# Sums of squares, norm spreads and bonus sums of a layer 0 projection in array tiles of a quarter

## What is computed

```python
qkv = silu(causal_dwconv(f[..., :1536], conv_w))          # 12 blocks of 128 channels: q, k, v
q, k = l2norm(heads(q, 128)) * 128 ** -0.5, l2norm(heads(k, 128))
f = f + (f_prev - f) * mu                                  # r, k, v, wd, ad, gd of the other group
w_log = -softplus(-(w0 + tanh(wd) @ w2)) - 0.5             # lora of the decay
a = sigmoid(a0 + ad @ a2)                                  # lora of the gate
kk = l2norm(heads(k * k_k, 64))
k = k * (1 + (a - 1) * k_a)
bonus = sum(r_h * k_h * r_k, axis=-1) * v_h
```

## Time and profile before

| | |
|---|---|
| median of 3 runs | 1567.32 us (1565.9 to 1569.51) |
| span of the profiled execution | 1565.6 us; its time beside the span is not listed apart |
| TensorE busy | 1492.0 us, 95% of the span |
| VectorE, ScalarE, POOL busy | 844.8, 666.4, 91.4 us |
| mean granted TensorE clock | 0.981 of 2.4 GHz |

### The profile page before, as it was taken

The page is one execution under the profiler, slowest core; times in us unless marked ns, Lnnn a source line. Parts: engine busy times, 40 slices in busy tenths (PEclk is TensorE's granted clock), DMA queues, the critical chain, the costliest instruction groups (busy, mean ns, idle before and its releaser), DMA issues.

```text
span 1565.6 us, 24908 instructions
## 1 busy us (share of the span) xinstructions
PE 1492.0 (95%) x9901; PEld 1243.9 (79%) x9901; DVE 844.8 (54%) x1400; ACT 666.4 (43%) x1156; POOL 91.4 (6%) x132
## 2 busy tenths in 40 slices
PE   5999998999999999999999997999989999999997
PEld 4776776887778888878888986988868888878886
DVE  4366546777676442334436626787746442334433
ACT  5543434445545442124334434676645442124331
POOL 0110013322300000000000002000000000000000
PEclk8999999999999999999999998999999999999999
DMA  6222200000152233322331241000042323322321
GB/s 224 81 70 78 81 14 14 2 2 2 55 189 76 99 94 110 95 81 94 108 122 55 81 139 64 2 2 3 2 135 68 93 93 110 95 81 94 108 81 54
DMA packets 32607, 119.38 MB, mean 76 GB/s; under 512 B 3696, under 2 KB 3824, under 8 KB 32496
## 3 DMA queue, kind: packets, MB, share of 16 engines
q1 hardware_dynamic: 29808, 108.84, 21.7%
q10 hardware_dynamic: 2688, 8.98, 1.6%
HBM read 115.71 MB, written 2.10 MB: 75 GB/s over the span
## 4 chain that ended last, share of the span: by engine, by line
PE 74%; DVE 8%; ACT 3%; issue 1%; DMA 0%; ACTq 0%; DVEq 0%; SPq 0%
PE bank L337 19%; PE bank L339 18%; PE bank L338 18%; PE bank L2543 2%; PE bank L2556 2%; PE bank L1136 2%; PE bank L2532 1%; PE bank L2533 1%; PE bank L1118 1%; PE bank L1082 1%; PE bank L2135 1%; DVE nmax L2613 1%; PE bank L1022 1%; PE bank L1126 1%; DVE ul_m L459 1%
## 5 line engine op out<-in xcount | busy, mean ns | idle before, releaser
L330 DVE TENSOR_TENSOR wl_m<-ring,wh_m 128x1024 fp32r<-128x1024 f32 x124 | 152.0, 1226 | 158.5 <-ACT wh_m L322 156.2
L337 PE MATMUL bank<-uh_m,wh_m 128*128 128x512 f32 (+2 forms) x576 | 216.5, 376 | 3.6 <-DVE ffo L1946 1.9
L338 PE MATMUL bank<-ul_m,wh_m 128*128 128x512 f32 (+2 forms) x576 | 216.0, 375 | 0.0
L339 PE MATMUL bank<-uh_m,wl_m 128*128 128x512 f32 (+2 forms) x576 | 216.0, 375 | 0.0
L322 ACT ACTIVATE wh_m<-ring 128x1024 fp32r<-128x1024 f32 x124 | 131.6, 1061 | 192.2 <-PE bank L339 189.7
L337 PE MATMUL bank<-wh_m,hh 128*128 128x512 f32 x448 | 174.4, 389 | 0.0
L338 PE MATMUL bank<-wl_m,hh 128*128 128x512 f32 x448 | 174.3, 389 | 0.0
L339 PE MATMUL bank<-wh_m,hl 128*128 128x512 f32 x448 | 174.3, 389 | 0.0
L1936 DVE TENSOR_TENSOR hraw<-hraw 128x512 f32<-128x512 f32 x64 | 44.3, 693 | 166.7 <-ACT hraw L1892 166.6
L1892 ACT ACTIVATE hraw<-bank 128x512 f32<-128x512 f32 x64 | 38.3, 598 | 214.8 <-PE bank L339 214.8
L337 PEld LDWEIGHTS bank<-uh_m,wh_m 128*128 128x128 f32 x576 | 108.6, 189 | 24.9 <-issue 2.7
(11 more groups left out here) (418 smaller groups left out, 2809.1 us busy)
## 6 DMA issues: line engine op xcount, KB each, us to landing
ring<-in_wstream_dram SPq DMA_DIRECT2D x200, 512.0 KB, 3.5
rowbuf<-in_rows_dram ACTq DMA_DIRECT2D x6, 512.0 KB, 3.8
xres<-in_x_dram SPq DMA_DIRECT2D x4, 512.0 KB, 6.7
xres<-in_x_dram ACTq DMA_DIRECT2D x1, 2048.0 KB, 10.0
out_dram<-xres ACTq DMA_DIRECT2D x4, 512.0 KB, 4.5
prerow<-in_rows_dram ACTq DMA_DIRECT2D x3, 512.0 KB, 4.9
con<-in_consts_dram SPq DMA_DIRECT2D x1, 869.5 KB, 13.3
par<-in_params_dram SPq DMA_DIRECT2D x1, 680.5 KB, 11.7
```

Source lines behind the costliest of these rows:

```text
L330: v.sig(v.e.tensor_tensor(dn[3][:, c % RING, :], slot(c), dn[2][:, c % RING, :].bitcast(F32), ALU.subtract), sem("w_lo"), it * per + c + 1)
L337: pe.matmul(out, lh, rh, start=start, stop=False)
L338: pe.matmul(out, lh, rl, start=False, stop=False)
L339: return pe.matmul(out, ll, rh, start=False, stop=stop)
```

## The change

- The two loras run in two blocks, in front of chunks 4 and 5. Each has two gate products on the rows 64 to 127 of the array and two decay products on the rows 0 to 63 by turns, in four banks. The gate's sigmoid and the decay's sum are made in halves, in steps 4 and 5, and the decay's sigmoid in step 6.
- The squares run in three groups, in front of chunks 10, 19 and 23: four products of 32 columns of weights, each into another quarter of the partitions of the bank. ScalarE puts the squares in four buffers that are free then (the values' slots, and the bonus operand's), and waits for a sum only once in four. Roots and reciprocals run on 128 partitions in place of 8; lines without a sum hold a root of eps.
- The key norms' spreads run as one group in front of chunk 15, into banks 7, 4, 5 and 6: four products of 32 rows with the high halves, then four with the low ones. Those of q and k are such a group each, in front of chunks 27 and 28. The eight rows of the selector that POOL copied shrink to three, from a new constant.
- The bonus sums are four products of 32 columns (`bonus_sums`, in front of chunk 12) that leave the sums with time along the columns. ScalarE copies them to SBUF (step 12, behind `root_hi`), four transposes turn them (`turn_bonus`, in front of chunk 13), and VectorE copies the columns that count in step 14.
- `turn_ba`, the gate steps and sums move one chunk later, and VectorE's `normed` of the keys too.

The diff, cut to its core:

```diff
-        sq = xres[:, 2, :].rearrange("p (b t) -> p b t", b=2)
+        bT = xres[:, 2, 0:T]
-        LW_BANK = (5, 6, 7, 4)
+        ALORA_BANK, LW_BANK = (4, 5, 4, 5), (6, 7, 6, 7)
+        KEY_BANK = (7, 4, 5, 6)
+        def sq(j):
+            return rk[:, j - 8, :] if j >= 8 else F(VRB + j % 4)
+        def quad(q):
+            return slice(32 * q, 32 * q + 32)
...
         def proj0_pe(pe):
+            def loras(i):
+                if i == 0:
...
+                    pe.wait_ge(sem("wd_tanh"), 1)
+                else:
+                    pe.wait_ge(sem("a_done"), i)
+                    pe.wait_ge(sem("lw_in"), i)
+                for b in (i, i + 1):
+                    pe.matmul(bank[ALORA_BANK[b]][:, :], PR("w2a2")[64:128, b * P:(b + 1) * P], fT[64:128, WA, PAD:],
                               start=True, stop=True).then_inc(sem("a_ready"), 1)
+                    pe.matmul(bank[LW_BANK[b]][:, :], fT[0:64, WA, PAD + b * P:PAD + (b + 1) * P], PR("w2a2")[0:64, :],
                               start=True, stop=True).then_inc(sem("lw_ready"), 1)
...
+            def squares(g):
+                pe.wait_ge(sem("sq_done"), 4 * g + 4)
...
+                window = C("rows2") if g == 0 else C("row")[:, g - 1:g + 31]
+                for q in range(4):
+                    ins = pe.matmul(bank[6 if g == 0 else 7][quad(q), :], window, sq(4 * g + q), start=g < 2, stop=g != 1)
+                ins.then_inc(sem("ss_ready"), 1)
+            def spread_norms(g):
+                if g < 2:
+                    pe.wait_ge(sem("inv_norm"), g + 1)
+                if g == 0:
                     pe.wait_ge(sem("by_pool"), 1)
                     pe.wait_ge(sem("gate_step"), 5)
                     pe.wait_ge(sem("bonus_sb"), 1)
+                for n in (nrh, nrl):
+                    for q in range(4):
+                        if n is nrh and g:
+                            pe.wait_ge(sem("normed"), 4 if g == 1 else 5 + q)
+                        ins = pe.matmul(bank[KEY_BANK[q] if g == 0 else 4 + q][:, :], spread[quad(q), g, :], n[quad(q), :], start=n is nrh, stop=n is nrl)
+                        if n is nrl:
+                            ins.then_inc(sem("spread"), 1)
+            def bonus_sums():
                 pe.wait_ge(sem("rk_done"), 4)
+                pe.wait_ge(sem("gate_step"), 2)
+                for b in range(4):
+                    ins = pe.matmul(bank[4][quad(b), :], C("rows2"), rk[:, b, :], start=True, stop=True)
+                ins.then_inc(sem("bonus_ready"), 1)
+            def turn_bonus():
+                pe.wait_ge(sem("bonus_ready"), 2)
                 for i in range(NT):
+                    ins = pe.transpose(bank[4][:, i * P:(i + 1) * P], bT[:, i * P:(i + 1) * P], ident)
                 ins.then_inc(sem("bonus_ready"), 1)
...
         def proj0_dve(v):
...
+                if p == 14:
+                    e.wait_ge(sem("bonus_ready"), 3)
+                    e.tensor_copy(bonus[:, :, :].rearrange("p i (b c) -> p i b c", c=2),
+                                  bank[4][:, :].rearrange("p (i b x) -> p i b x", i=NT, b=4)[:, :, :, 15:17]).then_inc(sem("bonus_sb"), 1)
+                if 15 <= p < 19:
+                    normed(p - 15)
...
         def proj0_pool(g):
+            e.wait_ge(sem("con_loaded"), 16)
+            e.tensor_copy(spread[:, 0, :].rearrange("p (h c) -> p h c", h=2), C("quad")[:, 0:2].unsqueeze(2).to_broadcast([P, 2, 64]))
+            e.tensor_copy(spread[:, 1:3, :], C("quad")[:, 0:3:2].unsqueeze(2).to_broadcast([P, 2, P])).then_inc(sem("by_pool"), 1)
...
         def proj0_act(a):
...
                 if p == 11:
-                    gate_exps()
                     root(1)
                 if p == 12:
+                    gate_exps()
                     root_hi(1)
+                    e.wait_ge(sem("bonus_ready"), 1)
+                    e.activation(bT, bank[4][:, :], ACT.Copy).then_inc(sem("bonus_ready"), 1)
```

More of the change, by code:

```diff
@@ L70 @@
 CONST_PARTS = [("ident", P), ("eps", 4), ("ones", P), ("strict", P), ("incl", P), ("bones", P), ("cum", 2 * P),
-               ("pairs", P), ("same", (LEVELS - 1) * 64), ("row", 31), ("rows2", 32), ("neg", P), ("cmask", NT * NCMP), ("cneg", NT * NCMP),
+               ("pairs", P), ("same", (LEVELS - 1) * 64), ("row", 36), ("quad", 3), ("rows2", 32), ("neg", P), ("cmask", NT * NCMP), ("cneg", NT * NCMP),
                ("ifreq", HALF), ("hsel", 4)]
@@ L197, in program @@
         early = ExitStack()
-        spread = sb("spread", [P, 12, P], F32R, c=early)
-        nr = sb("nr", [8, T], c=early)
+        spread = sb("spread", [P, 3, P], F32R, c=early)
+        nr = sb("nr", [P, T], c=early)
         early.close()
@@ L578, in gate_sums @@
                 pe.matmul(bank[5][:, 16:32].rearrange("p (i h) -> p i h", i=NT), ones, gs[:, :, 0, :], start=True, stop=True).then_inc(sem("gate_step"), 1)
[L580 to L588, removed]
+            def squares(g):
+                pe.wait_ge(sem("sq_done"), 4 * g + 4)
+                if g == 0:
+                    pe.wait_ge(sem("lw_in"), 4)
+                elif g == 1:
+                    pe.wait_ge(sem("normed"), 1)
+                window = C("rows2") if g == 0 else C("row")[:, g - 1:g + 31]
+                for q in range(4):
+                    ins = pe.matmul(bank[6 if g == 0 else 7][quad(q), :], window, sq(4 * g + q), start=g < 2, stop=g != 1)
+                ins.then_inc(sem("ss_ready"), 1)
@@ L621, in proj0_pe @@
                     gate_sums()
-                if p == R0 + 6:
-                    bonuses()
-                if R0 + 7 <= p < R0 + 11:
-                    spread_norm(p - R0 - 7)
-                if CONV0 + 4 <= p < CONV0 + 12:
-                    squares(4 + p - CONV0 - 4)
+                    squares(0)
+                if p == 12:
+                    bonus_sums()
+                if p == 13:
+                    turn_bonus()
+                if p == 15:
+                    spread_norms(0)
@@ L628, in proj0_pe @@
+                if p in (19, 23):
+                    squares(1 if p == 19 else 2)
                 weights(pe, p)
@@ L637, in z_products @@
                     if c < NTB + 2:
-                        for j in range(4):
-                            spread_norm(4 + 4 * (c - NTB) + j)
+                        spread_norms(1 + c - NTB)
                     weights(pe, c)
@@ L675, in conv, with log_decay @@
                     v.link(ins) if i < 3 else ins.then_inc(sem("conv_done"), 1)
-            def log_decay():
-                for i in range(NT):
+            def log_decay(first):
+                for i in (first, first + 1):
                     e.wait_ge(sem("lw_ready"), i + 1)
@@ L800, in key_norm, with a_gate @@
                 square(b, kkT[:, b, :])
-            def a_gate():
-                for b in range(4):
+            def a_gate(first):
+                for b in (first, first + 1):
                     e.wait_ge(sem("a_ready"), b + 1)
-                    e.activation(aT[:, b, :], bank[4 + b][:, :], ACT.Sigmoid, bias=PR("a0")[:, b:b + 1]).then_inc(sem("a_done"), 1)
+                    e.activation(aT[:, b, :], bank[ALORA_BANK[b]][:, :], ACT.Sigmoid, bias=PR("a0")[:, b:b + 1]).then_inc(sem("a_done"), 1)
             def log_decay():
```

90 lines of the change are left out of this document (31 added, 59 removed).

## The result

The changed kernel took 1548.79 us (median of 5 runs, 1545.11 to 1552.19), the kernel before 1566.91 us on the same chip (median of 5). The ratio is 0.9875 with a 95% interval of 0.986 to 0.989. The forecast of 1546.3 us is 0.9866 of the 1567.32 it started from, inside that interval.

A forecast was written before the change was run, and what follows sets the result against it. TensorE was taken as the bound, with insertions between projection chunks paid in full. Savings 3.4 + 10.5 - 0.1 + 1.4 - 0.45 + 6.2 = 20.95 us off the median 1567.3 gave 1546.3 us (chance 0.42), range 1542 to 1555.

The forecast's parts named there:

- Loras: Two blocks in front of chunks 4 and 5, four passes each, 2.2 us a block: saved 3.4 us.
- Squares: Twelve single squares become three groups of 1.27 us, four column quarters running at once: saved 10.5 us.
- rival 2: Square and spread groups: quarters run two at a time, 3.9 us more, 1550.2 us; chance 0.11.
- rival 3: Column tiles run one after another, a square group 3.77 us, three cost 7.5 more, 1553.8 us; chance 0.08.
- Gates: Gate steps one chunk later, behind chunk 8; VectorE's operand ready about when TensorE is through chunk 9: -0.1 us.
- Key spreads: One group of 0.76 us in front of chunk 15, plus 0.45 wait for the bonus copy: saved 1.4 us.
- Bonus: Chunks 12 to 14: wait 0.35, idle 3.3 before chunk 13, saved 1.2, clock fall loses 1.65: -0.45 us.
- rival 1: No fall of the clock at chunk 13: 1.65 us more saved, 1544.7 us; chance 0.27.
- Chunks 27 and 28: Two spread groups of 0.76 us, wait of 1.3 stays, both half-clock falls go: saved 6.2 us.
- rival 5: VectorE becomes the bound in four chunks, 0.5 us each, 1548.3 us; chance 0.08, shared with a later wait.
- The term that failed: Behind chunk 28 the order is unchanged and begins earlier by the whole saving, so the sum comes off the median.

The follow-up runs named there:

- the squares on the whole array: Changed kernel with square groups 2 and 3 sent to all 128 columns, all but one of zero weight, in place of quarters: 1551.49 us, ratio to before 0.9889.
- The spreads on the whole array: Changed kernel with each norm spread on 128 rows, selectors zero outside their quarter, in place of row quarters: 1553.06 us, ratio to before 0.9905.

## Why the prediction was right, and by what it was off

The direction and nearly all of the size were right, and by the right steps; what was missing is a term for the clock behind the projection. The predicted saving in the projection was 20.95 us and 21.0 were measured. An agreement that close is luck: two small errors in the bookkeeping, below, balance in it, and the second profile of the changed kernel saves 193.95 - 174.11 = 19.8. Before's 193.95 is known from one profile. By the medians the whole saving is 18.1 us in the result and 19.4 where the changed kernel ran again. In the prediction's unit, the distance of chunk starts less 5.44:

- **Loras**: 2.2 a block predicted, 2.14 measured (47.77 - 40.32 - 5.44 = 2.01, and 0.13 that the next start is late). Saved 3.5; the experiment that put them apart gave 3.7 in the projection.
- **Squares**: 1.27 a group predicted, 1.23 measured. Saved 10.6 of the predicted 10.5. Four quarters run at once; rival 2 (two at a time) and rival 3 (one after another) fall. What one after another costs, the experiment shows: 2.25 more a group, where rival 3 had 2.5.
- The rule of the Trainium skill ("TensorE: Matmul & The Clock Gate", "The mechanism") that a weight load overlaps matmuls in flight only when the row group differs, taken as the prediction takes it (column groups one after another), does not agree here: column quarters share their row groups, the group in front of chunk 12 loads its weights from 96.40 to 96.56 while its first products, 0.62 long from 96.41, are in flight, and eight instructions took 1.07 us against 3.60 on the whole array. The measurement decides.
- **Gates**: chunk 10 shows no wait; 0 where -0.1 was predicted.
- **Key spreads**: a group costs 0.90, not 0.76, and its wait for the bonus copy is 0.6 with the tail, not 0.45. Together 1.5 in place of 1.2. But the four of before cost 2.8, since the first was the 0.85 that the bonus part used and not 0.66. Saved 1.3 where 1.4 was predicted.
- **Bonus**: the wait in front of chunk 12 is 0.34 (predicted 0.35); the idle in front of chunk 13 is 3.12 (3.3), ends on ScalarE's copy, and has one half-clock stretch of 3.4 us behind it, as predicted. Chunks 12 and 13 are late by 1.49 + 3.82 + 1.71 = 7.0 up to chunk 14 against 6.7: -0.3 for the predicted -0.45. The size of that stretch was luck: six profiles of the study have that idle in front of chunk 13, and in one the stretch is 3.4 long, in four 6.8, and in one there is none (the squares on the whole array), which is rival 1. So the size of this term depends on the execution, 0, 1.6 or some 2.8 us; the forecast had chances for the first two and none for the last.
- **Chunks 27 and 28**: both falls are gone as predicted, and the kept wait is 1.2. Saved 5.95 of 6.2; the difference is the group's 0.90. The spreads on the whole array had no fall behind them either, at 1.9 us a group, so the shorter stretch was not needed for it there; the reason given for the falls (products on 8 rows) fits this, but one profile of each kernel does not show it.
- **VectorE** (rival 5) did not become the bound: chunks 16 to 18 start 5.44 apart.

These sum to 3.5 + 10.6 + 1.3 - 0.3 + 5.95 = 21.05, the measured 21.0. **The term that failed** is the last sentence of the sum, "Behind chunk 28 the order is as before and begins that much earlier": the order is, but the clock isn't. The profiled execution gave 3.4 us back there, the repeated one 0.3. Over all profiles of the study the rest took 1340.7 to 1345.5, and the three at 1345.36 and above are those with two stretches of 6.8 us. The range's 2 us each way "for falls elsewhere" were the right kind of allowance, but less than the 3.4. Whether the changed kernel falls into the longer stretches more often than before stays open: before has one profile here, and of its other runs only the time and the mean clock are on record.

The three waits of the change were foreseen one by one, as was their sum of some 4 us, but they were taken as given. That they can be had back, 5.8 to 7.0 us, by moving the consumers with the producers was shown afterwards.

## What to carry to other kernels

Small products that use a quarter of the array's columns or rows are worth grouping by four: here a group cost little more than one had. When such a group gathers several producers, write down for each consumer which operation on ScalarE or VectorE is last, and move the whole chain (sums, copy, transposes, spreads) by a step rather than one link. Time a change of a few us in the stretch where it acts, since the clock elsewhere moves an execution by as much.

## What was not expected of the hardware

- Four column quarters cost what one product did: 1.23 us a group against 1.19 for a single square; a group of row quarters, four spreads, cost 0.90 against 0.66 for a single one before.
- The order of the instructions in the program didn't set the order of their starts between array tiles: alternating high and low halves started as four high, then four low.
- Products on 8 rows had half clock behind them, and the same number of products on 128 rows, nearly all zeros, none; the insertions were equally long within 0.3 us. There is one profile of each, so this may be chance.
- The stretches of half clock behind identical work vary between executions of one kernel: at 230.2 and 295.1 us, 6.8 long each, in one profile, at 232.7 and 420.4, 3.4 each, in another, some 3 us of the whole time.
